# Moving the value loads of a decode attention stage from SyncE's DMA queue to GpSimd's

## The chip, the cores and the metric

The kernel runs on one core of a Trainium2 chip. The metric is the time of one execution of the whole program in microseconds (us) on the device. A core has TensorE (PE, matmuls and transposes), VectorE (DVE), ScalarE (ACT), GpSimd (POOL), SyncE (SP, which here only issues transfers) and 16 DMA engines that move data between HBM and on-chip memory. Transfers that SP issues appear in the profile as queue q1 (hardware_dynamic), those that GpSimd issues as queue q0 (software_dynamic).

## The reference

One inference step of two decoder layers, for a prompt of 512 tokens and for a sample group of 8 sequences with 8 new tokens each. What matters here is one part of the first layer, for the sample group: attention of the new tokens over a window of 2048 cached keys and values with three dilations. Cut to that part:

```
A_PATTERNS = ((128, 1), (512, 4), (2048, 16))     # window, dilation
def dilated_sample(q, kb, vb, slopes, window, dil, w_buf):
    T = q.shape[1]
    j = jnp.arange(window // dil + 1)
    idx = w_buf + jnp.arange(T)[:, None] - j[None, :] * dil
...
    kg, vg = kb[:, idx], vb[:, idx]
    s = jnp.einsum('bthd,btjhd->bthj', q, kg) * SCALE - slopes[:, None] * (j * dil).astype(jnp.float32)
    p, m, den = masked_softmax(s, valid[None, :, None, :])
    return jnp.einsum('bthj,btjhd->bthd', p, vg), (m + jnp.log(den))[..., 0]
...
    kab = jnp.concatenate([ca_k.astype(jnp.float32), ka], axis=1)
    vab = jnp.concatenate([ca_v.astype(jnp.float32), va], axis=1)
    o_a = combine_dilations([dilated_sample(qa, kab, vab, sl_a, w, d, w_a) for w, d in A_PATTERNS])
```

There are 16 heads of 64 elements and everything is float32, so that a cached token has 4 KB of keys and 4 KB of values.

## The kernel before

The program is a chain of stages, each a block of five engine programs with a barrier at its end. The stage that the change touches is `attend_sample_a`; in the profiled execution it runs from about 743 to 978 us. The stages ahead of it (projection and attention of the prompt) and behind it (`compress_sample` first) are the same in both kernels.

The stage goes through NB = 8 sequences, called batches (b) here. For each batch it loads only the cache rows that some dilation uses: NF = 5 blocks of keys and 5 blocks of values, each 128 partitions with 2048 float32, 1 MB (8 KB in a row in memory for each partition). I call them K(b,0) to K(b,4) and V(b,0) to V(b,4). All of them go through one **ring** of RING = 14 slots: load number `at = 10*b + n` (n = 0 to 4 keys, 5 to 9 values) goes into slot `at % 14`. A load may be issued only when the block 14 places earlier has been used: a key block when PE has transposed it (semaphore `turned`), a value block when PE has multiplied with it (`weighed`). Fourteen places back from V(b,0) to V(b,3) are K(b-1,1) to K(b-1,4); from V(b,4) it is V(b-1,0); from K(b,0) to K(b,3) it is V(b-2,1) to V(b-2,4), and from K(b,4) it is K(b-1,0).

PE's order in the stage is written out: for f = 0 to 4 it transposes K(b,f) (`keys`, L983, 16 transposes) and then computes the scores of the block before it (`scores`, L995). At f = 2 it also transposes the softmax weights of batch b-1 (`turn_weights`, L1010 and L1012), and at f = 3, after K(b,3), it multiplies them with V(b-1,0) to V(b-1,4) (`weigh`, L1023 for the new values and L1030 for the cached ones). DVE and ACT copy the transposed keys from PSUM (L1059), in turn. DVE makes no such copy before the constant tables `bias` (644 KB) and `own` (128 KB) are there (`bias_ready`), because the wait stands ahead of its loop.

SP issues every load of the stage, in this order for each batch: K(b,0) to K(b,4), for the first batch also `bias` and `own`, then the new values `v_new` (32 KB), then V(b,0) to V(b,4), then the store of batch b-2. It is one program: an issue that has to wait holds up all those behind it. GpSimd does nothing in this stage.

Of the kernel before, what the change touches and what calls it, by code (L numbers as in the profile page):

```python
# [21 lines left out]
NB = 8  # L22
# [440 lines left out]
class Norm:  # L463
# [14 lines left out]
    def load(self, sp):  # L478
        sp.dma_start(self.gain[:, :], self.gain_row.broadcast_to([P, D_MODEL])).then_inc(self.gain_ready, 16)
        sp.dma_start(self.bias[:, :], self.bias_row.broadcast_to([P, D_MODEL])).then_inc(self.gain_ready, 16)  # L480
# [400 lines left out]
def attend_sample_a(nc, z, cache_k, cache_v, o, ident, consts):  # L881
# [3 lines left out]
    NP, NF, NK, RING = HA // 2, 5, 10, 14  # L885
# [3 lines left out]
    kc, vc = (c.rearrange("e b (p r) h d -> (e b) p r (h d)", r=16) for c in (cache_k, cache_v))  # L889
    kl, vl = (c.rearrange("e b (a s q r) h d -> (e b) a s q (r h d)", s=2, q=4, r=2) for c in (cache_k, cache_v))  # L890
    with Space(nc, "sa") as s:
        ring = [s.sb(f"ring{i}", [P, 2, D_MODEL]) for i in range(RING)]
# [10 lines left out]
        bT = [s.bank(f"bT{w}") for w in range(4)]  # L903
        bS = [s.bank(f"bS{i}") for i in range(3)]
        bO = s.bank("bO")
        slot_in = [s.sem(f"slot_in{i}") for i in range(RING)]
        new_in, copied, stored = ([s.sem(f"{n}{u}") for u in range(2)] for n in ("new_in", "copied", "stored"))
        const_ready, bias_ready, zeroed, turned, scored, s_read, max_ready, exp_done = (
            s.sem(n) for n in ("const_ready", "bias_ready", "zeroed", "turned", "scored", "s_read", "max_ready", "exp_done"))
        den_ready, weighed, o_read, wide_ready, on_ready = (s.sem(n) for n in ("den_ready", "weighed", "o_read", "wide_ready", "on_ready"))  # L910
# [3 lines left out]
        def key_fill(b, f, i):  # L914
            return 2 + 20 * b + 4 * f + i + 3 * max(0, b - 1 if f <= 2 else b)
# [4 lines left out]
        def copies(n, e):  # L920

            return (n - e) // 2 + 1

        with nc.Block() as block:
            @block.sync
            def _(sp):
                sp.dma_start(q[:, :], qcols).then_inc(const_ready, 16)
                sp.dma_start(k_new[:, :], kcols).then_inc(const_ready, 16)

                def load(b, n, big, last):  # L930

                    at, slot = 2 * NF * b + n, ring[(2 * NF * b + n) % RING]
                    gone = at - RING
                    if gone >= 0:
                        gb, gn = divmod(gone, 2 * NF)
                        if gn < NF:
                            sp.wait_ge(turned, key_fill(gb, gn, 3) + 1)
                        else:
                            sp.wait_ge(weighed, NF * gb + gn - NF + 1)
                    f = n % NF  # L940
                    if f < 4:
                        sp.dma_start(slot[:, :, :], big[b, :, 2 * f:2 * f + 2, :]).then_inc(slot_in[at % RING], 16)
                    else:
                        sp.dma_start(slot[:, :, :].rearrange("p r c -> p (r c)"), last[b, 96:128, 1, :, :]).then_inc(slot_in[at % RING], 16)

                def store(b):
                    sp.wait_ge(on_ready, b + 1)
                    sp.dma_start(o[SEQ + b * NT:SEQ + (b + 1) * NT, :].rearrange("t (h d) -> h t d", d=HD), on[b % 2][:, :]).then_inc(stored[b % 2], 16)

                for b in range(NB):  # L950
                    for n in range(NF):
                        load(b, n, kc, kl)
                    if b == 0:
                        sp.dma_start(bias[:, :], consts["bias_a_s"]).then_inc(bias_ready, 16)
                        sp.dma_start(own[:, :, :].rearrange("p h d -> p (h d)"), consts["own_head"]).then_inc(bias_ready, 16)
                    if b >= 2:
                        sp.wait_ge(weighed, NF * (b - 1))
                    sp.dma_start(v_new[b % 2][:, :], z[SEQ + b * NT:SEQ + (b + 1) * NT, VA:VA + D_MODEL]).then_inc(new_in[b % 2], 16)
                    for n in range(NF, 2 * NF):
                        load(b, n, vc, vl)  # L960
                    if b >= 2:
                        store(b - 2)
                for b in (NB - 2, NB - 1):
                    store(b)
                for u in range(2):
                    sp.wait_ge(stored[u], 16 * (NB // 2))

            @block.tensor
            def _(pe):
# [4 lines left out]

                def keys(b, f):
                    at = 2 * NF * b + f
                    pe.wait_ge(slot_in[at % RING], 16 * (at // RING) + 16)
                    for i in range(4):
                        bank = bank_free(key_fill(b, f, i))
                        for jj in range(2):  # L980
                            j = 2 * i + jj
                            for t in range(2):
                                last = nc.tensor.transpose(bank[:, (2 * jj + t) * P:(2 * jj + t + 1) * P],  # L983
                                                           ring[at % RING][:, t, j * P:(j + 1) * P], ident[:, :])
                        last.then_inc(turned, 1)
# [29 lines left out]
                def weigh(b):  # L1015
                    for e in range(2):
                        pe.wait_ge(copied[e], copies(weight_fill(b, 2), e))
                    pe.wait_ge(new_in[b % 2], 16 * (b // 2) + 16)
                    if b >= 1:
                        pe.wait_ge(o_read, b)  # L1020
                    for c in range(4):
                        rows, cols = slice(QUAD * c, QUAD * (c + 1)), slice(4 * HD * c, 4 * HD * (c + 1))
                        nc.tensor.matmul(bO[rows, 0:4 * HD], pT_new[:, rows], v_new[b % 2][:, cols], start=True, stop=False)  # L1023
                    for f in range(NF):
                        at = 2 * NF * b + NF + f
                        pe.wait_ge(slot_in[at % RING], 16 * (at // RING) + 16)
                        for t in range(2):
                            for c in range(4):
                                rows, cols = slice(QUAD * c, QUAD * (c + 1)), slice(4 * HD * c, 4 * HD * (c + 1))
                                last = nc.tensor.matmul(bO[rows, 0:4 * HD], pT[:, 2 * f + t, rows], ring[at % RING][:, t, cols],  # L1030
                                                        start=False, stop=(f == NF - 1 and t == 1))
                        last.then_inc(weighed, 1)

                pe.wait_ge(const_ready, 32)
                for n, x in enumerate((k_new, q)):
                    for j in range(NP):
                        last = nc.tensor.transpose(bT[n][:, j * TS:(j + 1) * TS], x[:, j * P:(j + 1) * P], ident[0:TS, 0:TS])
# [1412 lines left out]
```

## Time and profile before

| | us |
|---|---|
| median of 3 runs (2460.08 to 2462.71) | 2461.02 |
| the profiled execution | 2460.89 |
| its span in the profile | 2459.1 |
| of it the stage `attend_sample_a`, about | 743 to 978 |
| PE busy, whole span | 2196.6 (89%) |
| DMA queue q1 (issued by SP), share of 16 engines, whole span | 44.2% |
| DMA queue q0 (issued by GpSimd), share of 16 engines, whole span | 8.5% |
| median time from issue to landing, key blocks | 12.9 |
| the same, value blocks | 20.4 |

The profile comes from one execution. Views by stretch give the busy time of each engine, TensorE's granted clock as a share of full speed, and the mean busy share and rate of the DMA engines. Timelines give single instructions, or runs of like ones, and in brackets how long the engine was idle before and what ended that. "SPq" rows are issues by SP, "POOL ... DMA" rows issues by GpSimd; their duration is that of the issue, not of the transfer.

### The profile page before, as it was taken

What the parts mean: (1) busy time and instruction counts of PE and PEld (TensorE: products, weight loads), DVE (VectorE), ACT (ScalarE), POOL (GpSimd) and SP (SyncE); (2) the same over time, 40 slices, a digit from 0 to 9 for tenths busy, and PEclk for the clock granted to TensorE, in tenths of its full rate; (3) what the DMA queues carried; (4) which work ended last, traced back from release to release, by engine and by line L of the source; (5) the groups of instructions that cost most, each with busy time, mean ns of one, the idle gap of its engine ahead of it and who ended that gap; (6) DMA issues with size and microseconds to landing.
All of it is one profiled execution on the core that took longest, in us unless ns stands there. A gap on an engine that the chain in (4) does not pass through costs nothing. (4 is left out here: it accounts for less than half of the span.)

```text
span 2459.1 us, 34146 instructions
## 1 busy us (share of the span) xinstructions
PE 2196.6 (89%) x13530; PEld 1326.0 (54%) x13530; DVE 856.5 (35%) x2143; ACT 718.1 (29%) x1447; POOL 324.9 (13%) x403
## 2 busy tenths in 40 slices
PE   5999999888986887899499979879999999999798
PEld 3444456444444564788266634346666666666443
DVE  1000001155663443333344423225455463545222
ACT  0001000166662332121154420024434343443300
POOL 1000001034450000442333310000000000000000
PEclk8999999989998988899799989989999999999899
DMA  4223314021119996752444354069797988979710
GB/s 128 73 107 107 73 59 115 11 67 52 44 45 360 410 402 249 296 191 84 179 180 159 124 163 127 0 161 298 238 309 249 295 276 268 295 238 313 273 57 21
DMA packets 204525, 436.29 MB, mean 177 GB/s; under 512 B 56928, under 2 KB 160144, under 8 KB 187728
## 3 DMA queue, kind: packets, MB, share of 16 engines
q1 hardware_dynamic: 195728, 356.47, 44.2%
q0 software_dynamic: 8640, 77.64, 8.5%
q8 instruction: 108, 1.77, 0.3%
q14 instruction: 49, 0.40, 0.0%
HBM read 409.49 MB, written 163.13 MB: 233 GB/s over the span
## 5 line engine op out<-in xcount | busy, mean ns | idle before, releaser
L1881 PE MATMUL rec_bR<-x1T,rec_w 128*128 128x512 f32 x768 | 355.6, 618 | 0.0
L1881 PEld LDWEIGHTS rec_bR<-x1T,rec_w 128*128 128x128 f32 x768 | 147.4, 197 | 172.1 <-issue 171.1
L320 PE MATMUL pab_acc<-xT,pab_w 128*128 128x512 f32 x512 | 225.9, 601 | 14.5 <-DMA pab_w<-in_w_in_ab 14.5
L320 PEld LDWEIGHTS pab_acc<-xT,pab_w 128*128 128x128 f32 x512 | 97.7, 193 | 136.3 <-issue 121.4
L324 PE MATMUL pab_acc<-pab_w,xT 128*128 128x512 f32 (+1 forms) x384 | 155.7, 565 | 0.0
L643 ACT ACTIVATE ap_sc<-ap_sc,ap_nmax 128x128 f32<-128x128 f32 (+1 forms) x192 | 106.2, 554 | 85.2 <-DVE ap_nmax L673 84.0
L1219 PE MATMUL cmp_bH<-cmp_xT,cmp_w 128*128 128x256 f32 x512 | 130.6, 380 | 0.0
L822 PE MATMUL mab_acc<-mab_w,mab_hT 128*128 128x512 f32 x256 | 116.8, 616 | 13.9 <-DMA mab_hT<-scratch_h 13.9
L673 DVE CUSTOM_DVE_ANT_0 ap_sc<-ap_bS,ap_bias 128x128 f32<-128x128 f32 (+1 forms) x192 | 86.6, 488 | 112.5 <-DMA ap_bias<-in_bias_p 46.2
L2256 PE MATMUL out_acc<-out_w,oT 128*128 128x512 f32 x256 | 112.6, 602 | 13.2 <-DMA out_w<-in_w_out_c 13.2
L382 DVE COPY pab_xc<-pab_bC 64x256 f32<-64x256 f32 x8 | 3.4, 422 | 342.4 <-PE pab_bC L235 342.2
L983 PE MATMUL sa_bT<-ident,sa_ring 128*128 128x128 f32 x640 | 88.6, 298 | 35.5 <-DMA sa_ring<-in_cache_a_k 26.4
L2085 POOL TENSOR_TENSOR rec_v_own<-rec_rows,rec_row_own 64x512 f32<-64x512 f32 x16 | 16.5, 1034 | 780.0 <-PE rec_bX L1940 630.0
L1890 PE MATMUL rec_bR<-rec_w,x1T 128*128 128x128 f32 x1024 | 117.0, 275 | 0.0
L1890 PEld LDWEIGHTS rec_bR<-rec_w,x1T 128*128 128x128 f32 x1024 | 115.7, 192 | 0.5 <-issue 0.5
L324 PEld LDWEIGHTS pab_acc<-pab_w,xT 128*128 128x128 f32 x384 | 72.3, 190 | 79.9 <-issue 79.9
L983 PEld LDWEIGHTS sa_bT<-ident,sa_ring 128*128 128x128 f32 x640 | 79.0, 154 | 46.6 <-DMA sa_ring<-in_cache_a_k 29.9
L611 PE MATMUL ap_bT<-ident,ap_sc 128*128 128x128 f32 x480 | 74.7, 288 | 30.0 <-ACT ap_pT L658 18.4
L1210 PE MATMUL cmp_bT<-ident,cmp_xg 128*128 128x128 f32 x512 | 77.8, 278 | 22.3 <-POOL cmp_xg L1168 20.3
L611 PEld LDWEIGHTS ap_bT<-ident,ap_sc 128*128 128x128 f32 x480 | 53.7, 144 | 76.8 <-POOL ap_sc L707 69.0
L1254 DVE COPY cmp_xT<-cmp_bT 128x512 f32<-128x512 f32 x80 | 55.4, 692 | 110.3 <-PE cmp_bT L1210 110.3
L1059 DVE COPY sa_kT<-sa_bT 128x512 f32<-128x512 f32 x80 | 55.3, 692 | 104.9 <-PE sa_bT L983 92.2
(371 smaller groups left out, 3422.4 us busy)
## 6 DMA issues: line engine op xcount, KB each, us to landing
out<-in_cache_a_k SPq DMA_DIRECT2D x8, 8160.0 KB, 29.4
out<-in_cache_a_v SPq DMA_DIRECT2D x8, 8160.0 KB, 29.3
sa_ring<-in_cache_a_k SPq DMA_DIRECT2D x40, 1024.0 KB, 12.9
sa_ring<-in_cache_a_v SPq DMA_DIRECT2D x40, 1024.0 KB, 20.4
rec_w<-in_w_in_c SPq DMA_DIRECT2D x64, 512.0 KB, 6.8
pab_w<-in_w_in_ab SPq DMA_DIRECT2D x8, 2048.0 KB, 9.9
pab_w<-in_w_in_ab SPq DMA_DIRECT2D x64, 128.0 KB, 3.2
ap_bias<-in_bias_p SPq DMA_DIRECT2D x16, 512.0 KB, 4.1
```

The source lines that it names most:

```text
L320: last = nc.tensor.matmul(acc[j][:, :], w[u][:, k, j * P:(j + 1) * P], xT[:, k, 0:SEQ], start=(k == 0), stop=(k == KD - 1))
L324: last = nc.tensor.matmul(acc[j][:, 0:width], xT[:, k, j * P:(j + 1) * P], w[u][:, k, 0:width], start=(k == 0), stop=(k == KD - 1))
L611: last = nc.tensor.transpose(bT[h][:, j * P:(j + 1) * P], sc[(i - LAG) % RING][h][:, j * P:(j + 1) * P], ident[:, :])
L643: nc.scalar.activation(at, at, ACT.Exp, bias=nmax[:, i % RING, h:h + 1], scale=-1.0, accum_out=den[:, i % RING, h:h + 1]).then_inc(exp_don ...
L673: nc.vector.tensor_tensor_reduce(out=sc[i % RING][h][:, 0:cols], in0=bS[i % 2][h][:, 0:cols], in1=bias[grp % 2][:, h, SEQ - cols:SEQ], sca ...
L822: last = nc.tensor.matmul(acc[m % 2][half][:, :], hT[:, k, m * P:(m + 1) * P], w[:, k, 512 * half:512 * half + 512], start=(k == 0), stop= ...
L983: last = nc.tensor.transpose(bank[:, (2 * jj + t) * P:(2 * jj + t + 1) * P], ring[at % RING][:, t, j * P:(j + 1) * P], ident[:, :])
L1210: last = nc.tensor.transpose(bT[f % 4][:, j * P:(j + 1) * P], xg[u][:, g, k * P:(k + 1) * P], ident[:, :])
L1219: last = nc.tensor.matmul(bH[i % 2][:, 0:KVB * P], w1[i % 2][:, k, :], xT[i % 2][:, k, :, :].rearrange("p g n -> p (g n)"), start=(k == 0) ...
L1881: last = nc.tensor.matmul(bank[:, :], w[h % 2][:, at, k, :], xT[:, k, 0:SEQ], start=(k == 0), stop=(k == KD - 1))
L1890: last = nc.tensor.matmul(bank[:, m * P:(m + 1) * P], xT[:, k, m * P:(m + 1) * P], w[h % 2][:, V_AT, k, :], start=(k == 0), stop=(k == KD ...
L2256: last = nc.tensor.matmul(acc[m % 2][half][:, :], oT[:, k, m * P:(m + 1) * P], w[:, k, 512 * half:512 * half + 512], start=(k == 0), stop= ...
```

## The change

The value loads V(b,n) leave SP's program and make up a program of GpSimd, in the same order and with the same waits on `turned` and `weighed`. SP keeps the key loads, the tables, `v_new` and the stores. Each slot of the ring gets two semaphores in place of one, for keys and for values, and PE waits for the one that fits; the count is the number of loads of that kind into that slot so far. The 14 semaphores for values are kept to the program's end and not cleared with the stage's others. Nothing changes in size, number or placement of the loads, nor in the programs of PE, DVE and ACT otherwise.

```
+        def wait_part(pe, at):
+            pe.wait_ge(slot_in[is_value(at)][at % RING], 16 * sum(is_value(x) == is_value(at) for x in range(at % RING, at + 1, RING)))
+
+        def load(engine, b, n, big, last):
...
                 for b in range(NB):
                     for n in range(NF):
-                        load(b, n, kc, kl)
+                        load(sp, b, n, kc, kl)
...
                     sp.dma_start(v_new[b % 2][:, :], z[SEQ + b * NT:SEQ + (b + 1) * NT, VA:VA + D_MODEL]).then_inc(new_in[b % 2], 16)
-                    for n in range(NF, 2 * NF):
-                        load(b, n, vc, vl)
                     if b >= 2:
                         store(b - 2)
...
+            @block.gpsimd
+            def _(pool):
+                for b in range(NB):
+                    for n in range(NF, 2 * NF):
+                        load(pool, b, n, vc, vl)
+
...
-                    pe.wait_ge(slot_in[at % RING], 16 * (at // RING) + 16)
+                    wait_part(pe, at)
```

SP's program around batches 0 to 3, before. `sa_ring<-in_cache_a_k` is a key block, `sa_ring<-in_cache_a_v` a value block; the L944 row of each kind is block 4:

```order
L942 DMA sa_ring<-in_cache_a_k 128x2048 x4
L944 DMA sa_ring<-in_cache_a_k 128x1x2048
L954 DMA sa_bias<-in_bias_a_s 128x1288
L955 DMA sa_own<-in_own_head 128x256
L958 DMA sa_v_new<-scratch_z 8x1024
L942 DMA sa_ring<-in_cache_a_v 128x2048 x4
L944 DMA sa_ring<-in_cache_a_v 128x1x2048
L942 DMA sa_ring<-in_cache_a_k 128x2048 x4
L944 DMA sa_ring<-in_cache_a_k 128x1x2048 [waits sa_turned]
L958 DMA sa_v_new<-scratch_z 8x1024
L942 DMA sa_ring<-in_cache_a_v 128x2048 [waits sa_turned] x4
L944 DMA sa_ring<-in_cache_a_v 128x1x2048 [waits sa_weighed]
```

The same place of SP's program now, in the new kernel's line numbers:

```order
L943 DMA sa_ring<-in_cache_a_k 128x2048 x4
L945 DMA sa_ring<-in_cache_a_k 128x1x2048
L961 DMA sa_bias<-in_bias_a_s 128x1288
L962 DMA sa_own<-in_own_head 128x256
L965 DMA sa_v_new<-scratch_z 8x1024
L943 DMA sa_ring<-in_cache_a_k 128x2048 x4
L945 DMA sa_ring<-in_cache_a_k 128x1x2048 [waits sa_turned]
L965 DMA sa_v_new<-scratch_z 8x1024
L943 DMA sa_ring<-in_cache_a_k 128x2048 [waits sa_weighed] x4
```

The value rows have gone from between the key rows. GpSimd's program at the same place, from the last stage before to its first value loads:

```order
L458 DMA out<-scratch_z 64x128 x4
L458 DMA out<-scratch_z 8x8x128 x2
L558 UNCONDITIONAL_BRANCH [waits moved]
L973 UNCONDITIONAL_BRANCH [waits barrier_Pool_Activation_PE_DVE_SP_gather]
L943 DMA sa_ring<-in_cache_a_v 128x2048 x4
L945 DMA sa_ring<-in_cache_a_v 128x1x2048
L943 DMA sa_ring<-in_cache_a_v 128x2048 [waits sa_turned] x4
L945 DMA sa_ring<-in_cache_a_v 128x1x2048 [waits sa_weighed]
```

Before, the row behind the branch on the barrier was already that of the next stage's gather; now 40 value loads stand between, in their old order among themselves.

## Rows read from the trace of the kernel before

**Rows 1.** Busy time of each engine in stretches of 20 us, the stage's middle and end

```profile
core 0: us, PE busy (x) PEld busy (x) DVE busy (x) ACT busy (x) POOL busy (x), PEclk, DMA share, GB/s
765.00:785.00 20.00, 16.92 (x181) 12.87 (x182) 9.65 (x19) 5.60 (x10) 0.00 (x0) 0.91 1.02 420
...
845.00:865.00 20.00, 15.59 (x202) 11.00 (x199) 6.51 (x14) 4.44 (x7) 0.00 (x0) 0.91 1.01 419
...
945.00:965.00 20.00, 16.84 (x229) 11.50 (x227) 8.48 (x19) 6.12 (x12) 0.00 (x0) 0.96 0.64 258
```

**Rows 2.** Waits of the stage: who waited for whom, total us, times, longest

```profile
POOL cmp_x L1182 <- POOLq L82: 241.3, 1, 241.3
...
PE sa_bT L983 <- DMA sa_ring<-in_cache_a_k: 26.4, 8, 4.4
```

**Rows 3.** DMA queues of 765 to 950 us: packets, MB, rate

```profile
DMA packets 11108, 75.34 MB, mean 407 GB/s; under 512 B 1919, under 2 KB 1919, under 8 KB 1975
## 3 DMA queue, kind: packets, MB, share of 16 engines
q1 hardware_dynamic: 11089, 75.06, 99.8%
```

**Rows 4.** PE's timeline: start, duration, instructions, idle before and its end

```profile
780.98 1.97 PE L983 MATMUL sa_bT<-ident,sa_ring 128*128 128x128 f32 x16 [2.89 <-DMA sa_ring<-in_cache_a_k]
...
791.03 1.91 PE L983 MATMUL sa_bT<-ident,sa_ring 128*128 128x128 f32 x16
...
794.44 4.52 PE L1030 MATMUL sa_bO<-sa_ring,sa_pT 128*32 128x256 f32 x80
...
806.05 3.46 PE L983 MATMUL sa_bT<-ident,sa_ring 128*128 128x128 f32 x16 [4.20 <-DMA sa_ring<-in_cache_a_k]
...
951.31 4.52 PE L1030 MATMUL sa_bO<-sa_ring,sa_pT 128*32 128x256 f32 x80
```

**Rows 5.** SP's issues around the end of the first weighing

```profile
795.57 0.55 SPq L944 DMA_DIRECT2D sa_ring<-in_cache_a_v  x1
796.43 2.92 SPq L942 DMA_DIRECT2D sa_ring<-in_cache_a_k  x4
799.41 0.55 SPq L944 DMA_DIRECT2D sa_ring<-in_cache_a_k  x1
800.01 0.48 SPq L958 DMA_DIRECT2D sa_v_new<-scratch_z  x1
800.54 1.93 SPq L942 DMA_DIRECT2D sa_ring<-in_cache_a_v  x4
```

**Rows 6.** Both DMA queues at once, 165 to 168 us: packets, MB, share

```profile
q0 software_dynamic: 206, 0.83, 67.0%
q1 hardware_dynamic: 205, 0.42, 36.0%
```

**Rows 7.** Timeline of all engines at the stage's start

```profile
743.73 0.49 SPq L927 DMA_DIRECT2D sa_q<-scratch_z  x1
...
764.44 1.29 DVE L1059 COPY sa_kT<-sa_bT 128x512 f32<-128x512 f32 x2 [11.98 <-DMA sa_own<-in_own_head]
...
765.19 1.12 PE L983 MATMUL sa_bT<-ident,sa_ring 128*128 128x128 f32 x4 [9.09 <-DVE sa_kT L1059]
```

**Rows 8.** The first load of the stage (sa_q, 256 KB): from issue to landing

```profile
DMA to landing us min/median/max: 3.6/3.6/3.6
```

**Rows 9.** GpSimd's timeline: issues of transfers in other stages

```profile
159.98 0.81 POOL L450 DMA_DIRECT2D out<-kv  x1
...
392.87 1.21 POOL L427 DMA_DIRECT2D pab_first<-in_cmp_w_v  x1 [19.22 <-PE pab_bC L246]
...
979.37 1.07 POOL L1182 DMA_INDIRECT cmp_x<-in_cache_b_cmp_k,page_idx  x1 [241.28 <-POOLq L82]
```

**Rows 10.** First packets after an issue: 744:745, 162:163, 394:395 and 983:984 us

```profile
q1 hardware_dynamic: 2, 0.01, 3.6%
...
q0 software_dynamic: 2, 0.01, 2.0%
...
q0 software_dynamic: 9, 0.04, 32.6%
...
q0 software_dynamic: 2, 0.03, 9.4%
```

More of the change, by code:

```diff
@@ L905, in attend_sample_a @@
         bO = s.bank("bO")
-        slot_in = [s.sem(f"slot_in{i}") for i in range(RING)]
+        slot_in = [[s.sem(f"keys_in{i}") for i in range(RING)], [s.pool_dma_sem(f"values_in{i}") for i in range(RING)]]
         new_in, copied, stored = ([s.sem(f"{n}{u}") for u in range(2)] for n in ("new_in", "copied", "stored"))
@@ L922, in copies, with is_value @@
             return (n - e) // 2 + 1
+        def is_value(at):
+            return int(at % (2 * NF) >= NF)
+        def wait_part(pe, at):
+            pe.wait_ge(slot_in[is_value(at)][at % RING], 16 * sum(is_value(x) == is_value(at) for x in range(at % RING, at + 1, RING)))
+        def load(engine, b, n, big, last):
+            at, slot = 2 * NF * b + n, ring[(2 * NF * b + n) % RING]
+            gone = at - RING
+            if gone >= 0:
+                gb, gn = divmod(gone, 2 * NF)
+                if gn < NF:
+                    engine.wait_ge(turned, key_fill(gb, gn, 3) + 1)
+                else:
+                    engine.wait_ge(weighed, NF * gb + gn - NF + 1)
+            f = n % NF
+            ready = slot_in[is_value(at)][at % RING]
+            if f < 4:
+                engine.dma_start(slot[:, :, :], big[b, :, 2 * f:2 * f + 2, :]).then_inc(ready, 16)
+            else:
+                engine.dma_start(slot[:, :, :].rearrange("p r c -> p (r c)"), last[b, 96:128, 1, :, :]).then_inc(ready, 16)
         with nc.Block() as block:
@@ L928, in _ @@
                 sp.dma_start(k_new[:, :], kcols).then_inc(const_ready, 16)
[L930 to L944, printed above, removed]
                 def store(b):
@@ L1025, in weigh @@
                         at = 2 * NF * b + NF + f
-                        pe.wait_ge(slot_in[at % RING], 16 * (at // RING) + 16)
+                        wait_part(pe, at)
                         for t in range(2):
```

## The prediction

> **What bounds the kernel now.** The stages are divided by barriers, and the change touches one, so I read the views of that stage alone, from 743 to 978 us; what it gains or loses moves the end by as much. The first view is the busy time by stretches [rows 1]: from 765 to 945 us the DMA engines show a busy share of about 1.0 at some 410 GB/s, in the middle stretch 1.01, while PE is busy for 15.6 to 16.9 us of 20. The stage is bound by its bytes, and the share falls only in the last stretch, 0.64, when the loads have run out. The second is the list of waits [rows 2]: PE waits for a key block 8 times, 26.4 us together, and GpSimd sits at the barrier for 241.3 us, so nothing else is on the engine that gets the loads. PE's timeline [rows 4] shows where those waits lie: once per batch, ahead of K(b,0), 2.89 us at 780.98 and 4.20 us at 806.05. The weighing of batch 0 starts at 794.44 and that of batch 6 at 951.31, so a batch takes (951.31 - 794.44) / 6 = 26.15 us. Ten blocks of 1.049 MB at the mean rate of 407 GB/s [rows 3] are 2.58 us each, 25.8 us in all: the batch is as long as its bytes. PE's own work is some 22 us of it.
>
> **What must stay in view** is the loop that hangs on the ring. The first four key blocks of batch b+1 wait for the slots of V(b-1,1) to V(b-1,4), so they are issued only during a weighing: SP issues V(1,4) at 795.57 and K(2,0) to K(2,3) from 796.43 [rows 5], right after the weighing that starts at 794.44. The next weighing comes only when PE has had K(2,3). From one weighing to the next there is therefore a chain: issue of K(b+1,0), landing of four key blocks, the PE work on the last of them, the weighing. Before, this chain has slack, since on a queue served in order only V(b,4) and what is left of the values before it lie ahead of the keys, and V(b+1,0) to V(b+1,3) lie behind them, issued from 800.54 on [rows 5]. So the four key blocks arrive one every 2.58 us and PE waits for the first alone.
>
> **The change, part 1: the values run beside the keys.** In the new order GpSimd waits with V(b,4) for the same event, the first product of a weighing, and then issues V(b+1,0), V(b+1,1) and V(b+1,2) at once, whose key slots are long free; V(b+1,3) follows after K(b,4). Five value blocks are thus in q0 just as four or five key blocks enter q1. How the two queues share the engines is seen where both are busy [rows 6]: 206 packets of q0 and 205 of q1 in 3 us, so packet against packet, and q0 got twice the bytes only since its packets were twice as long (0.83 MB against 0.42). Here both kinds of block have runs of 8 KB per partition, so I take half the bytes for each. The Trainium skill, page "DMA: Bandwidth & Descriptors", section "Queues, rings and completion order", lets an engine go round its queues too, but a whole packet of some 9 to 17 descriptors at a time; both readings give halves here.
>
> A key block then takes 2 x 2.58 = 5.15 us while values are queued, and four take 20.6 us. The chain by its parts: 0.2 us from the freed slot to the issue of K(b+1,0) (the second product of the weighing ends about 794.44 + 2 x 0.90 = 796.24, issue at 796.43 [rows 4, 5]); 2.9 us of fixed delay (`sa_q`, 0.26 MB, landed after 3.6 us [rows 8], of which 0.7 is its bytes); 20.6 us; then from the start of K(b,3) to the start of the cached values 794.44 - 791.03 = 3.41 us, and two of the five products, 2 x 0.90 = 1.80 us [rows 4]. Sum 28.9 us.
>
> From this comes off the time in which the keys are alone because q0 starts later. SP's first packets show within 1.3 us of the issue at 743.73 [rows 7, 10]. GpSimd's issues at 392.87, 159.98 and 979.37 had their first packets about 2.0, 2.9 and 4.5 us later [rows 9, 10], so 0.7 to 3.2 us more. V(b,4) is issued one product, 0.9 us, ahead of K(b+1,0), so the keys have 0 to 2.3 us alone, and each such us of full rate takes one off the 20.6. I take 1.0, nearest to the direct load and the direct store, since the third is an indirect gather. **Period 27.9 us against 26.15; six periods, + 10.5 us** (from + 2.7 at 2.3 us alone to + 16.5 at none). The DMA engines then idle for some 2 us per batch. A page figure by itself: the same page gives first bytes after about 1 us from GpSimd and 0.6 us from SP (section "Latency and other measured facts"); by it the keys would never be alone, and the sum would be 6 us more than mine.
>
> **Part 2: the start.** DVE waits for `own`, which lands at 764.44, and PE goes on at 765.19 after 9.09 us of idling [rows 7]. Ahead of it on SP's queue are 0.5 MB of q and k_new, five key blocks and `bias`: 6.56 MB with itself. Before, nothing else was in the way. Now five value blocks, 5.24 MB, compete as well. q0 starts some 3 us in, when q1 has had 1.2 MB; the other 5.3 MB at half rate take 5.3 / 0.2035 = 26.0 us. So `own` lands at about 745 + 3 + 26 + 2 of delay = 776, 11.6 us later. What comes back: K(1,0) to K(1,3) then have the engines for themselves and are there when PE needs them, so the 2.89 us wait at 780.98 [rows 4] goes. **Net + 8.7 us** for the weighing of batch 0. Its values have long been in. Bounds: + 5 if q0 takes less than half, + 12 if the wait stays.
>
> **Part 3: the rest.** GpSimd's 40 issues at 0.81 to 1.21 us [rows 9] are covered by its 241.3 us of waiting [rows 2]; the burst of four takes under 5 us and its blocks are first used a batch later. Without that cover they would cost some 40 us, but nothing in the stage wants GpSimd. SP loses 40 issues of about 0.5 us [rows 5]: its next key issue comes up to 0.6 us earlier, though the slot is what it waits for; nothing gained. The additional semaphores are no instructions on PE. The tail from the weighing of batch 6 stays as it is. Total 8.7 + 10.5 = **+ 19.2 us** on 2460.9 us (profiled) or 2461.0 (median), so **2480.2 us**. Of that + 7.7 to + 28.5 are the added bounds, about 2469 to 2489.
>
> **The rivals.**
> *Faster: the keys overtake the values.* Before, K(b+1,0) waits behind V(b,4) and some of V(b,3): issue 796.43, use 806.05, 9.6 us. If GpSimd's queue always started so late, or got so small a share (0.3 or less), that the keys passed at nearly full rate, K(b+1,0) would be there 3 to 4 us sooner. The bytes still bound the batch, at 25.8 against 26.15 us, and what is gained is at most 2 us over six batches, then the start, where a share of 0.3 costs little and saves the 2.89 us wait, and the last batch, whose values no longer count ahead of its keys: one or two blocks, 2.6 to 5 us. About 2453. It decides from a share under some 0.35. Against it speak the equal packets [rows 6].
> *No change.* The engines are full before [rows 1], and if the keys' chain of 28.9 us were shortened to the 25.8 of the bytes by a late q0, with the start's loss made good, the time would be 2459 to 2465. The Trainium skill says the like: the same page, section "Issuing engines are not separate DMA queues", holds that issuing from several engines only saves issue time, since all run on the same 16 engines.
> *Much slower.* PE now waits some 2 us ahead of each of K(b,1), K(b,2) and K(b,3) too. Before, a wait of 4.20 us was followed by 16 transposes in 3.46 us in place of 1.97 [rows 4], the granted clock going down. Should the clock be down when K(b,3) arrives, the 5.2 us behind it become 8 or more: 6 x 3 = 18 us on top, about 2498. The short waits speak against it: one of 2.89 us at 780.98 was followed by 1.97 us. The same sign would have a fall of the joint rate with both queues active.
> *The change doesn't do what it says*, that is, values still wait behind keys: the two programs share no wait, so I give this no more than the no-change case holds.
>
> **How the numbers follow.** Two runs differ by less than 0.2%, 5 us, only by chance, and that is the bound of "same". My case has 0.65, its own range 2469 to 2489; no change 0.1; faster 0.1; much slower 0.15. The range goes from 2462, within the no-change case, to 2493, into the slower one. Slower by over 0.2%: 0.8; same 0.1; faster 0.1.
>
> **What would show it.** Right: periods of the weighings near 28 us, PE waiting 1 to 2.5 us before each of K(b,0) to K(b,3) in place of 3 to 4 before K(b,0) alone; DMA share below 1 in the middle of the stage; key blocks landing some 5 us apart, q0 and q1 with equal packets; `own` landing near 776. Wrong: DMA share still 1.0 with a period of 26 (then the delay of q0 was mis-sized), or an `own` that lands before 770 (then the halves are wrong). If the transposes behind the short waits last 3 us, the clock is what I missed.

## The result

The changed kernel takes 2504.97 us (median of 4 runs, 2500.63 to 2512.14) against 2460.91 us before. The ratio is 1.0181, 95% interval 1.0156 to 1.0206: 44 us slower. The forecast was 2480.2 us in a range of 2462 to 2493, so the sign was right and the size was off by more than a factor of two.

The profiled execution of the changed kernel has a span of 2510.3 us, 51.2 more than before (its own time of 2512.14 is the highest of the four). Where they go is read from three events of the stage in both traces: SP's first issue (743.73 before, 747.20 after), the start of the first weighing and of the seventh, and the first issue of the next stage (978.66 and 1025.96).

| piece of the stage | before, us | after, us | difference |
|---|---|---|---|
| first issue to the weighing of batch 0 | 50.71 | 60.75 | + 10.0 |
| six batches (weighing 0 to weighing 6) | 156.9 (26.15 each) | 189.4 (31.56 each) | + 32.5 |
| weighing of batch 6 to the next stage | 27.35 | 28.64 | + 1.3 |
| the stage | 234.93 | 278.76 | + 43.8 |

The other 7.4 us lie ahead of the stage and behind it (3.5 and 3.9), where nothing was changed; the profiled run is also 7 us above the median. The 43.8 us of the stage are the 44 us of the medians.

PE's timeline of the changed kernel for one batch, to be laid beside [rows 4]:

```profile
807.95 4.52 PE L1041 MATMUL sa_bO<-sa_ring,sa_pT 128*32 128x256 f32 x80
...
820.51 3.54 PE L994 MATMUL sa_bT<-ident,sa_ring 128*128 128x128 f32 x16 [5.14 <-DMA sa_ring<-in_cache_a_k]
...
825.50 1.97 PE L994 MATMUL sa_bT<-ident,sa_ring 128*128 128x128 f32 x16 [0.34 <-DMA sa_ring<-in_cache_a_k]
...
830.49 3.60 PE L994 MATMUL sa_bT<-ident,sa_ring 128*128 128x128 f32 x16 [2.02 <-DMA sa_ring<-in_cache_a_k]
...
836.27 1.91 PE L994 MATMUL sa_bT<-ident,sa_ring 128*128 128x128 f32 x16
...
839.68 4.52 PE L1041 MATMUL sa_bO<-sa_ring,sa_pT 128*32 128x256 f32 x80
...
997.32 4.52 PE L1041 MATMUL sa_bO<-sa_ring,sa_pT 128*32 128x256 f32 x80
```

K(2,0), K(2,1) and K(2,2) are taken up 5.0 us apart, as they would be at half the rate. The waits of the stage, to be laid beside [rows 2]: PE now waits for key blocks 19 times, 49.1 us in place of 26.4, and GpSimd spends its time at the waits of the ring. The row shown is that for the weighings; another 61.1 us were for PE's transposes.

```profile
POOL sa_ring L945 <- PE sa_bO L1041: 169.3, 7, 25.9
...
PE sa_bT L994 <- DMA sa_ring<-in_cache_a_k: 49.1, 19, 5.6
```

The DMA engines, full before, now have pauses: their mean busy share from 765 to 950 us is 0.84. Busy time by stretches of 20 us (beside [rows 1]), and the queues of 765 to 950 us (beside [rows 3], 75.34 MB at 407 GB/s):

```profile
core 0: us, PE busy (x) PEld busy (x) DVE busy (x) ACT busy (x) POOL busy (x), PEclk, DMA share, GB/s
...
805.00:825.00 20.00, 14.86 (x198) 10.38 (x196) 6.10 (x12) 3.78 (x8) 2.61 (x5) 0.91 0.72 290
825.00:845.00 20.00, 17.64 (x223) 12.68 (x213) 6.66 (x14) 5.63 (x10) 2.09 (x4) 0.91 0.72 282
845.00:865.00 20.00, 12.94 (x134) 9.71 (x134) 7.65 (x16) 5.87 (x10) 0.53 (x1) 0.83 1.01 423
```

```profile
DMA packets 9433, 63.04 MB, mean 341 GB/s; under 512 B 1583, under 2 KB 1711, under 8 KB 1887
## 3 DMA queue, kind: packets, MB, share of 16 engines
q1 hardware_dynamic: 5262, 32.46, 42.5%
q0 software_dynamic: 4155, 30.35, 41.2%
```

The keys, which PE needs next, now land later than the values, which it needs a batch later. Before, the medians were 12.9 us for keys and 20.4 for values; after:

```profile
sa_ring<-in_cache_a_v POOLq DMA_DIRECT2D x40, 1024.0 KB, 14.6
sa_ring<-in_cache_a_k SPq DMA_DIRECT2D x40, 1024.0 KB, 20.0
```

What the forecast had not foreseen is in the 4 us after the ring's slots come free. First the issues, GpSimd's V(1,4) and V(2,0), then SP's K(2,0) to K(2,3):

```profile
809.34 0.53 POOL L945 DMA_DIRECT2D sa_ring<-in_cache_a_v  x1 [14.97 <-PE sa_bO L1041]
809.86 1.56 POOL L943 DMA_DIRECT2D sa_ring<-in_cache_a_v  x3
```

```profile
809.94 2.92 SPq L943 DMA_DIRECT2D sa_ring<-in_cache_a_k  x4
```

Then the DMA queues in the stretches 809 to 813.5 us and 813.5 to 813.75 us (packets, MB, share). The first packet of q1 comes 3.6 us after SP's issue, when q0 has moved 112 + 14 = 126 packets, nearly one value block, which is 8 packets for each of 16 engines:

```profile
q0 software_dynamic: 112, 0.92, 59.5%
...
q0 software_dynamic: 14, 0.11, 100.7%
q1 hardware_dynamic: 1, 0.01, 7.7%
```

From there on the two move equally many packets. The stretch 820 to 830 us:

```profile
q0 software_dynamic: 289, 2.11, 50.6%
q1 hardware_dynamic: 289, 2.10, 50.4%
```

The other five batches show the same: both queues are empty when the slots come free, and q1's first packets come 3.6 to 3.8 us after SP's issue, with about 1 MB of q0 ahead of them.

### The profile page after: what moved, and what is told of

Same layout as the page of the kernel before. It is cut to its first block and busy times, and to the rows that moved or that the text cites. A ratio compares the mean times of both kernels' runs of the same rounds, so it can differ in the third digit from the quotient of the medians.

```text
span 2510.3 us, 34146 instructions
## 1 busy us (share of the span) xinstructions
PE 2218.2 (88%) x13530; PEld 1339.8 (53%) x13530; DVE 856.4 (34%) x2143; ACT 718.1 (29%) x1447; POOL 344.9 (14%) x443
## 5 line engine op out<-in xcount | busy, mean ns | idle before, releaser
L994 PE MATMUL sa_bT<-ident,sa_ring 128*128 128x128 f32 x640 | 96.4, 314 | 63.4 <-DMA sa_ring<-in_cache_a_k 49.1
L994 PEld LDWEIGHTS sa_bT<-ident,sa_ring 128*128 128x128 f32 x640 | 85.3, 163 | 76.7 <-DMA sa_ring<-in_cache_a_k 56.5
L1070 ACT COPY sa_kT<-sa_bT 128x512 f32<-128x512 f32 x80 | 46.9, 586 | 172.6 <-PE sa_bT L994 172.5
```

Of the source, the lines that this page charges most:

```text
L1070: copy(kT[(NF * b + f) % 3][:, 2 * i:2 * i + 2, :].rearrange("p j k -> p (j k)"), bT[n % 4][:, :]).then_inc(copied[e], 1)
```

## The experiments

"First weighing" is the time from SP's first issue of the stage to the weighing of batch 0, "batch" the mean of the six batches after it, both from the profile, which is of one execution. Ratios are to the kernel before on the same chip, so times of kernels measured on different chips are best compared by their ratios. The expectations set two theories against each other. Theory A is always that the loss comes from two queues sharing the engines, in some of them with the queue that was issued first going first. Theory B differs from one experiment to the next, and each expectation says what it is.

| kernel | ratio (95% interval) | first weighing | batch | stage |
|---|---|---|---|---|
| before | 1 | 50.7 | 26.15 | 234.9 |
| changed | 1.0181 (1.0156 to 1.0206) | 60.8 | 31.56 | 278.8 |
| signals alone | 0.9999 (0.9987 to 1.0011) | 52.0 | 26.0 | 235.7 |
| batch 0's values on GpSimd | 1.0020 (1.0006 to 1.0033) | 60.1 | 25.6 | 241.1 |
| the others' values on GpSimd | 1.0148 (1.0125 to 1.0171) | 59.2 | 31.5 | 275.7 |
| everything on GpSimd | 1.0001 (0.9985 to 1.0016) | 51.6 | 26.0 | 235.6 |
| keys on GpSimd, values on SP | 1.0097 (1.0081 to 1.0114) | 51.0 | 30.0 | 258.1 |
| V(b,4) later by two products | 1.0051 (1.0034 to 1.0069) | 60.2 | 26.7 | 247.8 |
| V(b,4) after the weighing | 1.0051 (1.0033 to 1.0068) | 59.8 | 25.8 | 243.3 |
| values on ScalarE's queue | 1.0185 (1.0166 to 1.0204) | 60.3 | 31.2 | 275.0 |
| values as 2 x 4 KB runs | 1.0040 (1.0023 to 1.0056) | 58.2 | 26.1 | 242.3 |
| changed, tables first | 1.0162 (1.0142 to 1.0182) | 59.8 | 31.6 | 275.3 |
| V(b,4) late, tables first | 1.0035 (1.0021 to 1.0049) | 57.5 | 26.2 | 241.7 |
| one queue, both orders | 0.9982 (0.9968 to 0.9995) | 49.6 | 25.2 | 228.2 |
| one queue, tables first | 0.9987 (0.9977 to 0.9997) | 52.2 | 25.5 | 233.0 |
| one queue, V(b,4) late | 0.9968 (0.9952 to 0.9984) | 47.8 | 25.4 | 227.5 |
| values in two halves of partitions | 1.0535 (1.0513 to 1.0558) | 75.2 | 43.1 | 363.5 |

### The signals alone

SP issues everything in the old order; only the pairs of semaphores stay.

```
+                    for n in range(NF, 2 * NF):
+                        load(sp, b, n, vc, vl)
...
-            @block.gpsimd
-            def _(pool):
...
```

> Separate signals alone: all loads are issued by SP in the old order, with one semaphore per slot for keys and one for values. Both theories of the slow-down lie in the DMA queues, so both expect no change: 2461 us within 3, batches of 26.15 us, key block 0 of a batch used 9.6 us after its issue. If the signals cost anything, the time rises here too.

2462.29 us against 2462.25. The signals cost nothing.

### The start alone and the loop alone

In one kernel only batch 0's values are issued by GpSimd, in the other only those of batches 1 to 7; SP issues the remaining ones in their old place. The main edit is one condition, and SP's and GpSimd's programs ask it for each load:

```
+        def by_pool(at):
+            return int(NF <= at < 2 * NF)                      # the start alone
...
+            return int(at % (2 * NF) >= NF and at >= 2 * NF)    # the loop alone
```

> Only the five value blocks of the first batch go through GpSimd, the other 35 through SP in the old order. This is the start term alone: the table own should land some 28 us after its issue in place of 15.4, and the weighing of batch 0 should start 60 to 61 us after the stage's first issue in place of 50.7; batches of 26.15 us after it. About 2471 us by both theories. The delay may also be partly made good later if the ring then runs with more blocks in store (down to 2461).

The first weighing is 9.4 us later, as expected, but the time rises by 0.2% only, about 5 us, since the batches behind it are faster (25.6 us): with a single queue from then on, part of the delay is made good.

> The value blocks of batches 1 to 7 go through GpSimd, those of batch 0 through SP. This is the loop alone: start as before (weighing of batch 0 after 50.7 us), then batches of 31 to 32 us as in the changed kernel, 2461 + 6 x 5.4 = 2493 us by both theories. If the late first packet of the keys needs the full backlog of the start, batches stay under 28 us.

Batches of 31.5 us: the loop's loss needs no backlog from the start. But the first weighing was not as before, against what was expected. It came 8.5 us later although `own` landed as early as before, and PE's timeline says why:

```profile
789.53 3.47 PE L999 MATMUL sa_bT<-ident,sa_ring 128*128 128x128 f32 x16 [8.27 <-DMA sa_ring<-in_cache_a_k]
```

This is K(1,0), which PE awaited for 2.89 us before. GpSimd's V(1,0) and the next, issued from 771.27 us on, run beside the keys of batch 1, which stand on SP's queue behind the values of batch 0. So there was a loss at the start that the prediction had not named. It also puts the time, 2501.92 us, above the 2493 that were expected. The two kernels' losses, 0.20% and 1.48%, make up 1.81% within the intervals, but they don't divide it into start and loop, since the second kernel has a loss of 8.5 us at its own start.

### Everything on GpSimd

```
+        def by_pool(at):
+            return 1
...
+                    for n in range(2 * NF):
+                        if by_pool(2 * NF * b + n):
+                            load(pool, b, n, *((kc, kl) if n < NF else (vc, vl)))
```

> All 80 blocks go through GpSimd's queue, keys and values in the old order; SP keeps the tables, the new values and the stores. Theory A, the loss comes from two queues sharing the engines: gone here, 2459 to 2465 us, batches of 26.2 us, DMA share near 1. Theory B, GpSimd's queue by itself moves or signals these blocks more slowly: the loss stays or grows, 2490 us or more.

2462.15 us against 2462.25, batches of 26.0 us. GpSimd's queue alone does the same work in the same time, and theory B, that this queue is slower by itself, falls. What costs 44 us is that there are two queues.

### Roles exchanged

```
+        def by_pool(at):
+            return int(at % (2 * NF) < NF)
```

> Roles exchanged: the 40 key blocks go through GpSimd's queue, the 40 value blocks through SP's, with the same waits. Theory A, the queue whose transfer is issued first gets a whole block through before the other's first packet: V(b,4) on SP is still issued 0.6 us ahead of K(b+1,0), so the keys' first packet again comes some 3.8 us after the issue and batches stay at 31 to 32 us. Theory B, it is GpSimd's queue that goes first whatever the order: the keys now go first, are used some 6 to 7 us after their issue, and batches take 27 to 28.5 us. The start differs from the changed kernel's, since bias and own stand ahead of the values on SP and no key block is ahead of them.

Batches of 30.0 us, between theory A's 31 to 32 and B's 28.5 at most, and closer to A. Now SP's value block is issued first, at 827.65, and GpSimd's K(3,0) at 828.78:

```profile
827.65 0.55 SPq L945 DMA_DIRECT2D sa_ring<-in_cache_a_v  x1
```

```profile
828.78 0.53 POOL L943 DMA_DIRECT2D sa_ring<-in_cache_a_k  x1 [27.08 <-PE sa_bO L1046]
```

The queues from 828 to 833 us, one microsecond per group of lines: q1 has moved 2 + 16 + 46 + 53 = 117 packets, nearly a block, when q0's first show up.

```profile
q1 hardware_dynamic: 2, 0.02, 12.7%
...
q1 hardware_dynamic: 16, 0.13, 91.7%
...
q1 hardware_dynamic: 46, 0.38, 90.3%
...
q1 hardware_dynamic: 53, 0.43, 102.9%
...
q0 software_dynamic: 35, 0.29, 67.6%
q1 hardware_dynamic: 171, 0.12, 37.6%
```

So it isn't GpSimd's queue that goes first, but the queue whose transfer was issued first. K(3,0) is used at 837.68, 8.9 us after its issue in place of 10.6: SP issues its next value blocks only from 831.46 on, and from 832.5 to 834 us q0 alone moves data. So the batches are somewhat shorter than in the changed kernel. Here the start shows the other side: the tables have no key block ahead of them, and the first weighing is at 51.0 us.

### The values held back

```
-                    engine.wait_ge(weighed, NF * gb + gn - NF + 1)
+                    engine.wait_ge(weighed, NF * gb + gn - NF + 1 if n < NF else min(NF * gb + gn - NF + 3, NF * gb + NF))   # by two
...
+                    engine.wait_ge(weighed, NF * gb + gn - NF + 1 if n < NF else NF * gb + NF)                               # weighing
```

> As the changed kernel, but GpSimd issues V(b,4) two products of the weighing later (1.8 us), about 1.2 us after SP issues K(b+1,0), and V(b+1,0) to V(b+1,2) behind it. Theory A (first come, a whole block first): K(b+1,0) is now used 5.5 to 7 us after its issue in place of 10.6, batches take 27 to 28.5 us. Theory B (GpSimd's queue goes first whatever the order): the keys still start late, batches stay above 30 us. The start loss of 8 to 10 us stays by both.

> As the changed kernel, but GpSimd issues V(b,4) and what is behind it only after the whole weighing of batch b-1 (3.6 us later than in the changed kernel, 3 us after K(b+1,0)). Both theories let K(b+1,0) through alone: used 5.5 us after its issue. Halves for K(b+1,1) to K(b+1,3) after that: batches of 26.5 to 27.5 us, and 2475 to 2480 us with the start loss. If batches still take 31 us, the late first packet is not what lengthens them.

Holding back V(b,4), and with it the transfers behind it, by 1.8 us brings the batches from 31.56 to 26.7 us, and the ratio from 1.0181 to 1.0051 (2473.85 us). K(b+1,0) is used 5.4 to 7.0 us after its issue. With 3.6 us the batches of the profile are at 25.8, and the ratio is the same (2471.14 us). Both batches are a little shorter than was expected (27 and 26.5 us at least). From the kernel with 3.6 us, SP's issue of K(3,0) to K(3,3), GpSimd's of V(2,4), and PE's start on K(3,0), 6.2 us after SP's issue in place of 10.6:

```profile
834.85 3.06 SPq L943 DMA_DIRECT2D sa_ring<-in_cache_a_k  x4
```

```profile
837.70 0.53 POOL L945 DMA_DIRECT2D sa_ring<-in_cache_a_v  x1 [22.38 <-PE sa_bO L1041]
```

```profile
841.02 1.97 PE L994 MATMUL sa_bT<-ident,sa_ring 128*128 128x128 f32 x16 [0.75 <-DMA sa_ring<-in_cache_a_k]
```

Now the values' queue is the one that waits. In the batch before, GpSimd issued at 812.72 and q0's first packets are in the stretch 816.25 to 816.5. Theory A holds, and B, that GpSimd's queue goes first whatever the order, is excluded. What is left of the loss, 12 us, is the start, 9 us.

### A second hardware queue

ScalarE issues the values, between its copies, at the same events.

```
+                for n in range(NF, 2 * NF):
+                    load(act, 0, n, vc, vl)
...
+                        if f == 3 and 1 <= b < NB:
+                            load(act, b, 2 * NF - 1, vc, vl)
+                        if f == 3 and b + 1 < NB:
+                            for n in range(NF, NF + 3):
+                                load(act, b + 1, n, vc, vl)
+                        if f == 4 and b + 1 < NB:
+                            load(act, b + 1, NF + 3, vc, vl)
```

> The value blocks are issued by ScalarE in place of GpSimd, between its copies, at the same events; the queue is then a hardware one like SP's. Theory A (two queues share the engines, of whatever kind): batches of 28 to 32 us as in the changed kernel, about 2495 us. Theory B (a software queue beside a hardware one is the cause): the keys' first packet comes 1.3 us after the issue, batches take 28 us by the halves alone, about 2475 us. ScalarE's issues cost 40 x 0.5 us, beside its waits for PE.

2503.66 us and batches of 31.2 us, the same loss. ScalarE's queue (q10) had moved 114 packets by 807.75 us after its issue at 803.50, and the keys' first packets, issued at 804.36, came between 807.75 and 808 us. So the loss does not hang on the kind of queue.

### Shorter packets for the values

```
+            if is_value(at):
+                for t in range(2):
+                    part = big[b, :, 2 * f + t, :] if f < 4 else last[b, 96:128, 1, :, t * D_MODEL:(t + 1) * D_MODEL]
+                    engine.dma_start(slot[:, t, :], part).then_inc(ready, 16)
```

> As the changed kernel, but GpSimd issues each value block as two transfers of 0.5 MB whose runs are 4 KB, not 8. If the queues are served packet against packet, the keys now get two thirds of the bytes: a key block every 3.9 us in place of 5.15 while values are queued. If what goes ahead before the switch to the other queue is a fixed number of packets per engine (a block's 8), the keys' first packet comes about 1.3 us sooner too; if it is a fixed number of bytes, the lead stays. Batches: 31.6 - 3.8 x 1.3 - 1.3 = 25.4, thus 26.2 to 27 us by the bytes, or 26.7 to 27.5 with the full lead; own lands 6 us earlier than in the changed kernel. About 2468 us. If small runs make the transfers themselves slow, the rate of both queues together falls under 400 GB/s and batches stay above 29 us.

2468.8 us, batches of 26.1. The queues from 815 to 825 us:

```profile
q1 hardware_dynamic: 383, 2.75, 66.2%
q0 software_dynamic: 384, 1.43, 35.4%
```

Equal packets again, so two thirds of the bytes go to the keys, as expected. The head start is smaller too: 107 packets of 4 KB, 0.44 MB, by 808.75 us, and q1's first packets in the same microsecond, 2.7 us after SP's issue at 806.23. So it is not a fixed number of bytes. What was expected of `own` was wrong: DVE's wait for it was as long as in the changed kernel (20.5 us against 20.7).

### The tables first

```
                 for b in range(NB):
+                    if b == 0:
+                        sp.dma_start(bias[:, :], consts["bias_a_s"]).then_inc(bias_ready, 16)
+                        sp.dma_start(own[:, :, :].rearrange("p h d -> p (h d)"), consts["own_head"]).then_inc(bias_ready, 16)
                     for n in range(NF):
...
```

> As the changed kernel, but SP issues bias and own ahead of the first key blocks. If the start term is the late landing of own, the first weighing starts some 10 us earlier, 48 to 52 us after the stage's first issue in place of 60.7; batches stay at 31.5 us; about 2495 us, 10 less than the changed kernel. If the start is bound by the key blocks of batch 1, the gain is under 4 us.

2498.65 us, and the first weighing at 59.8 us, one us earlier only: the second case of the expectation, a start bound by the keys. DVE no longer waits for `own`, but PE's timeline shows key blocks at some 5 us each in its place:

```profile
764.94 3.67 PE L994 MATMUL sa_bT<-ident,sa_ring 128*128 128x128 f32 x16 [9.97 <-DMA sa_ring<-in_cache_a_k]
...
785.01 3.07 PE L994 MATMUL sa_bT<-ident,sa_ring 128*128 128x128 f32 x16 [2.03 <-DMA sa_ring<-in_cache_a_k]
...
795.22 3.04 PE L994 MATMUL sa_bT<-ident,sa_ring 128*128 128x128 f32 x16 [2.27 <-DMA sa_ring<-in_cache_a_k]
```

The start is bound by both, the table and the keys of the first two batches, which end nearly together.

> Both remedies together: GpSimd issues V(b,4) after the whole weighing, and SP issues bias and own first. Start at 48 to 52 us, batches of 25.8 us: 2459 us by the sum (2471 less 10 to 12 for the start). The DMA engines should then be full in the whole stage, so it can beat the kernel before by little, 2 to 5 us, if the last batch's keys no longer stand behind values; it can't if the bytes until the last key block are the same (2461).

Both remedies together give 2467.77 us where 2459 was expected, 0.35% above the kernel before. The loop is repaired (26.2 us), the start is not (57.5 us), and no run here repairs the start with two queues. None of the arrangements with two queues beat the one queue.

### One queue, other orders

SP issues everything. The two edits are the tables first, as above, and V(b,4) behind K(b+1,3), shown here. In the first kernel both are in, in the two others one each:

```
                     for n in range(NF):
+                        if b >= 1 and n == NF - 1:
+                            load(b - 1, 2 * NF - 1, vc, vl)
                         load(b, n, kc, kl)
...
-                    for n in range(NF, 2 * NF):
+                    for n in range(NF, 2 * NF - (b < NB - 1)):
                         load(b, n, vc, vl)
```

> The kernel before, all loads on SP, with two changes of order: bias and own ahead of the first key blocks, and V(b,4) issued behind K(b+1,3) in place of ahead of K(b+1,0). The first weighing starts at 46 to 48 us in place of 50.7, but the engines are full from the start on, so that brings nothing by itself; batches of 26.15 us; the keys of the last batch have one block less ahead of them, 2.6 us off: 2458 us. If the order inside a full queue doesn't matter at all, 2461.

> The kernel before with one change: bias and own ahead of the first key blocks. The engines are full from the start either way and the same bytes precede the last key block, so no change is expected: 2459 to 2461 us. If this is what made the kernel with both orders 0.18% faster, it shows 2456 to 2457.

> The kernel before with one change: V(b,4) issued behind K(b+1,3) in place of ahead of K(b+1,0). The last batch's keys have one block less ahead of them: 2.6 us off, 2456 to 2458 us. If order inside the full queue is worth nothing, 2460.

V(b,4) behind the keys alone gives 2454.46 us against 2461.64 on the same chip, a ratio of 0.9968 (0.9952 to 0.9984): 7 us faster than the kernel before, where 2.6 was expected, and the lowest ratio of this study. The tables first, from which nothing was expected, bring 0.13% by themselves, and both together no more than the one (0.9982); the three intervals overlap. Of the 7 us, 2.9 are at the first weighing (47.8 against 50.7), which the keys of batch 1 reach with one block less ahead of them. The expectation had put this block, 2.6 us, at the last batch; I take it for one and the same gain, made in batch 1 and kept. The rest is in batches of 25.4 in place of 26.15 us. The engines moved 415 GB/s from 765 to 950 us against 407 before [rows 3] and 410 in the kernel with the signals alone. Why the rate was higher is open: single batches vary between 23.4 and 29.6 us in the profiles of the one-queue kernels, and the kernels with old order and one queue show 26.0 (signals alone, everything on GpSimd).

### Values in halves of partitions

Each value block is two transfers of 64 partitions, in place of one of 128; runs stay at 8 KB.

```
+                for t in range(2):
+                    rows = slice(64 * t, 64 * t + 64)
+                    if f < 4:
+                        engine.dma_start(slot[rows, :, :], big[b, rows, 2 * f:2 * f + 2, :]).then_inc(ready, 16)
```

> As the changed kernel, but GpSimd issues each value block as two transfers of 64 partitions each, runs of 8 KB as before (4 packets per engine and transfer). The halves are the same as in the changed kernel by equal packets. If the head start of the queue that comes first is one transfer, it falls from 128 packets to 64, the keys' first packet comes 1.3 us sooner, batches 30.3 us, about 2497 us. If it is 8 packets per engine, it stays at 128 packets and batches at 31.5 us, about 2504 us.

This was to tell whether the head start is one transfer or 8 packets per engine, and it doesn't: the time rose to 2594.88 us, for another reason. The DMA engines are busy throughout and move much less. Busy time from 905 to 925 us:

```profile
905.00:925.00 20.00, 12.67 (x148) 8.54 (x152) 4.61 (x9) 2.34 (x4) 5.11 (x10) 0.83 1.01 246
```

Between 818 and 825 us, when q0 was alone, it moved 0.18 to 0.25 MB per us in place of 0.42. q0 was never empty when keys were issued, so the head start from two empty queues can't be read. One batch still shows something. SP issued K(2,0) at 820.07, with nothing of its own on the way, and from 820 to 825.5 us only q0 moved data:

```profile
q0 software_dynamic: 189, 1.19, 99.0%
```

A transfer of 64 partitions is 0.52 MB, so more than two of them went through after the issue, and 0.85 MB after 821.5. That is near the 8 packets per engine of the other kernels, and more than one transfer; but the rest of the transfer under way and one whole transfer behind it would be about as much. So the question stays open. Behind the head start the queues take turns, a wave of one packet for each of the 16 engines at a time. The half microseconds from 826, 826.5 and 827 us:

```profile
q1 hardware_dynamic: 15, 0.12, 111.8%
...
q0 software_dynamic: 16, 0.13, 81.8%
...
q1 hardware_dynamic: 16, 0.13, 107.9%
```

In the next batches small packets of SP's store were on the way when the keys were issued, and the delay was shorter there, some 3 us.

## Why the prediction was wrong

**The mechanism was right but for one step.** The chain from one weighing to the next became the bound; the values share the engines packet against packet (289 to 289); key blocks come 5.0 us apart where 5.15 was forecast; the DMA share falls below 1; the signals are worth nothing, and GpSimd's queue costs nothing when it is the only one. PE waits ahead of several key blocks, though not evenly: 4.3 to 5.6 us ahead of K(b,0), where 1 to 2.5 was forecast, then mostly ahead of K(b,2).

**The term that failed** is "from this comes off the time in which the keys are alone because q0 starts later ... I take 1.0". The keys are not alone at all, the values are. From the issue of K(b+1,0) to its use the prediction had 2.9 + 5.15 - 1.0 = 7.05 us; the trace has 820.51 - 809.94 = 10.57 in the batch shown, and 9.7 to 11.0, in the mean 10.3, in the six. That is 3.2 us more in each, 19 of the 22 us that the loop was undersized by (32.5 against 10.5). From K(b+1,0) to K(b+1,3) it is 15.76 us in the batch shown and 15.85 in the mean, forecast 15.45: 2.4 us more in six batches. The weighing's part is as forecast. The delay of GpSimd's queue was itself mis-sized: the three rows that I had gave 2.0 to 4.5 us, and here V(1,4)'s first packets came 1.2 to 1.4 us after its issue at 809.34. Nor was 1.0 us near the direct load and the direct store, as I wrote: by their rows the keys would be alone for none and 0.7 us. But that is the smaller part. By it alone the keys would have been alone for no time, and the period 28.9 us; the other 2.7 us are nearly all the first value block, which goes through before any of the keys.

**A rule was set aside that bore on it.** The Trainium skill, page "DMA: Bandwidth & Descriptors", section "Queues, rings and completion order", says that an engine drains a whole packet of some 9 to 17 descriptors from one ring before it changes over. I wrote that both readings give halves. In the long run they do; at the change-over they don't, and the chain goes through one change-over per batch. The trace agrees with neither reading throughout: about 8 packets of the profile per engine go first (126 in all), a little under the 9 to 17 of the Trainium skill, and behind them it is single ones in turn.

**The start** was forecast as + 8.7 us and is + 10.0, with `own` used 780.03 - 747.20 = 32.8 us after the first issue, forecast 32.3. That is near, but in part by luck, since the cause was only half of it: with the tables early the first weighing hardly moved (59.8 against 60.8), since the keys of batch 1 are as late.

**The rivals.** The much slower one named the clock; PE's transposes of K(b+1,0) did run at the lower clock (3.54 us for 16 at 820.51, 1.97 at 836.27), but the next block was not there before 825.50. In three of the six batches K(b+1,2) ran low too and K(b+1,3) was taken up without a wait. There K(b+1,0) to K(b+1,3) took 15.76 to 16.50 us; in the three others, where the blocks behind K(b+1,0) ran at full speed, it was 14.96 twice and 16.50 once. So the clock accounts for 4 us of the 32.5 at most, taking 14.96 as what the transfers alone would give. The faster rival and that of no change are excluded by the 44 us. The Trainium skill's sentence on issue time, beside the latter (page "DMA: Bandwidth & Descriptors", section "Issuing engines are not separate DMA queues"), doesn't hold for this stage: the second queue made it 43.8 us longer. The range was too narrow on the high side: I bounded only how late q0 starts, by rows in which one queue started at a time; none had both queues start within a microsecond from empty, as here in each batch, and I gave no bound for a late q1.

## What to carry to other kernels

In these runs two DMA queues shared the engines without regard to what was needed first. In a stage whose bytes fill the engines already, the second queue brought no bandwidth (423 GB/s in its fullest stretch against 420 before), and moved transfers that were needed late ahead of, or beside, those needed now. One queue in the order of need is a priority list; here a better order on it was worth 0.3% and a second queue cost 1.8%. If a second queue is needed, hold its transfers back by an event until the urgent ones have been issued (1.8 us of holding back brought a loss of 1.81% down to 0.51%).

## What the runs showed of the hardware

- When both queues are empty and two transfers are issued 0.6 to 1.1 us apart, the one issued first moves some 8 packets per engine (126, 117 and 114 packets of 8 KB on q0, q1 and q10; 107 and more of 4 KB) before the other's first packet, which comes 2.5 to 3.8 us after its own issue. Then they alternate packet by packet (waves of 15, 16 and 16 in turn in the kernel with halves of partitions). The 4 KB runs show that it isn't a fixed number of bytes. Whether the 8 are a count or the one transfer is open.
- A queue that joins a busy one also starts late: GpSimd's first packets came 3.5 to 4.0 us after the issue in the kernels that hold the values back, against 1.2 to 1.4 us on idle engines in the changed kernel (issue at 809.34, none before 810.5).
- Shares follow packets, not bytes: 4 KB runs against 8 KB runs gave 1.43 MB against 2.75 MB.
- Transfers into 64 partitions were half as fast as those into 128, with the engines shown as busy: 246 GB/s beside the keys' queue, 0.18 to 0.25 MB per us alone.
